# Second attention: key-query scores as two split products with stacked high and low parts

## The chip, the cores and the metric

The kernel runs on one core of a Trainium2 chip. The metric is device time in microseconds (us) of one execution. Five engines share the core: TensorE (PE, its weight loads are listed as PEld), VectorE (DVE), ScalarE (ACT), GpSimd (POOL) and SyncE (SP), which issues most of the DMAs.

## The reference, cut to what matters

The program is two transformer blocks on 512 positions. The second block has two causal attentions of eight heads each, head width 64: one with a forget gate whose cumulated logarithm is added to the scores, and a dilated one with distance penalties. The change touches their scores alone.

```python
def fox_attention(q, k, v, log_f):               # heads 12 to 19 of the kernel
    c = jnp.cumsum(log_f, axis=-1)
    ...
        s = jnp.einsum('bhqd,bhkd->bhqk', qb, k).astype(jnp.float32) * scale   # scale = 64 ** -0.5
        s = s + cq[..., :, None] - c[:, :, None, :]
        s = jnp.where(mask, s, NEG_INF)
        p = jax.nn.softmax(s, axis=-1)
        return jnp.einsum('bhqk,bhkd->bhqd', p.astype(v.dtype), v)

def dilated_window_branch(q, k, v, window, dilation, slopes):   # heads 20 to 27, three patterns in one pass
    s = jnp.einsum('bhrnqd,bhrnkd->bhrnqk', qs, kc).astype(jnp.float32) / math.sqrt(hd)
    ...
    bias = -slopes * (dilation * steps)
    s = jnp.where(valid, s + bias, NEG_INF)
```

A term that depends only on the query drops out of the softmax, so what is left of both biases is one number for each key and head.

## The kernel before

All arrays are fp32. Large projections are not computed as full fp32 products but split: each operand has a high part rounded to the format fp32r and a low part (the value less its high part), and three single-pass products high x high, high x low, low x high are added in one PSUM bank (line 1149). Scores, transposes and value products use full fp32 (lines 1288, 1301, 1317).

The order of all work is a written list, `STEPS`. Every engine walks through this list and does its own share of each step, in this order; semaphores join them. So what stands later in the list can't overtake on the same engine.

The second block's attention numbers its heads a = 12 + j, j = 0 to 15. It works on four query blocks of 128 (qb) and causal keys, so score row qb has (qb + 1) x 128 keys. Iteration j of the loop does, for i = 0 to 3:

- `X(a, i)`: TensorE transposes the probabilities of head a for key block i into a bank; ScalarE copies them to SBUF (line 1630).
- `S(a + 1, i)`: TensorE makes score row i of the next head (line 1288) and adds the mask (line 1290 or 1292); VectorE takes the row maximum (line 1956); ScalarE takes the exponential (line 1428). For heads 12 to 19 ScalarE also sums the row; for later ones VectorE multiplies by a table of counts and sums (line 1965).
- `W(a + 1, i - 1)`: VectorE divides by the row sum (lines 1966, 1967).
- `PV(a, i - 1)`: TensorE's product with the values (line 1317), accumulated over key blocks in one bank, `ob`.

Then follow, for j up to 11, a projection `qk2` (24 split products of 512 columns; the queries or the keys of a pair of heads two pairs ahead), `W(a + 1, 3)`, `PV(a, 3)` and `O(a)`, VectorE's copy of the head's output from `ob` (line 1977). The first value product of the next head waits for this copy:

```python
if kb == 0 and a > 0:
    pe.wait_ge(s_O, O_no[a] - 1)
```

ScalarE empties a `qk2` projection with two instructions, one for each head of the pair, into `Q2` (scaled by 1/8) or `K2`. These hold 65 rows for each of four slots: 64 of the head and one more, 1.0 in `Q2` and the key bias in `K2`, so that one product of 65 rows gives the score with its bias. The bias row comes by one DMA for each head on GpSimd's queue (`key_bias`, line 1010), four at the step `key_biases` ahead of the attention, later ones three to four heads ahead. GpSimd also makes the low parts of the weights for the projections (line 1000), ScalarE their high parts (line 1532, in an iteration behind the copy of transposed block 1).

Score rows and transposes take five PSUM banks in turn. Two banks alternate for projections; a projection waits until the one two before has been emptied.

After the attention come an output projection, a norm, the search for experts and 128 experts' products, which take the rest of the time.

Of the kernel before, what the change touches and what calls it, by code (L numbers as in the profile page):

```python
# [96 lines left out]
def build_schedule():  # L97
# [232 lines left out]
    def qk2(p, s):  # L330
        tile("qk2", 2 * p + s, KD, P)

    qk2(0, 0)
    qk2(0, 1)
    rows(12)
    qk2(1, 0)
    STEPS.append(("W", 12, TB - 1))
    qk2(1, 1)

    def out_part(f, k0, k1):  # L340
# [10 lines left out]
    for j in range(ATT2):  # L351
        a = 12 + j
        for i in range(TB):
            STEPS.append(("X", a, i))
            if j + 1 < ATT2:
                STEPS.append(("S", a + 1, i))
            STEPS.append(("L", a, i))
            if i:
                if j + 1 < ATT2:
                    STEPS.append(("W", a + 1, i - 1))  # L360
                STEPS.append(("PV", a, i - 1))
        if j // 2 + 2 < 8:
            qk2(j // 2 + 2, j % 2)
        if j == 13:
            out_part(0, 0, 3)
        elif j == 14:
            out_part(1, 0, 3)
            out_part(0, 3, 6)
        if j + 1 < ATT2:
            STEPS.append(("W", a + 1, TB - 1))  # L370
        STEPS.append(("PV", a, TB - 1))
        STEPS.append(("O", a))

        if j == ATT2 - 1:
            out_part(1, 3, 6)
        if j in (12, 13, 15):
            STEPS.append(("split", "o", *{12: (0, 3), 13: (3, 6), 15: (6, KD)}[j]))
# [47 lines left out]
def program(nc, t_in, out):  # L425
    build_schedule()
    ctx = ExitStack()
    with ctx:
# [71 lines left out]
        o += T  # L500
        Q2 = region(o, 4 * T, 4)
        rtmp = region(o, T)
# [17 lines left out]
        mq = region(o, 4 * T, 4)  # L520
        K2 = region(o, 4 * T, 4)
        o += 4 * T
# [46 lines left out]
        mv = region(mv_off, MB * T, MB)  # L569
        PT = region(PT_off, 4 * T, 4)  # L570
        hh = place("h_high", HH, [KD, T], F32R)
        hl = place("h_low", 4096, [KD, T], F32R)
# [77 lines left out]
        s_O = sem("head_outputs_done")  # L650
        s_kb = [sem(f"key_bias_in_buffer{i}") for i in range(4)]
        s_fmag = sem("forget_magnitudes_ready")
        s_fch = sem("forget_logs_done")
# [330 lines left out]
        def _(pool):  # L984
# [18 lines left out]
            def key_bias(j):  # L1003
                if j == 0:
                    pool.wait_ge(s_post, post_no[("forget", 0)])
                    pool.wait_ge(s_init2, 1)
                if j >= 4:
                    pool.wait_ge(s_S, s_no[(12 + j - 4, TB - 1)])
                src = zsm[j:j + 1, 2, :] if j < 8 else t_in["bias"][j - 8:j - 7, :]
                pool.dma_start(K2[NOPE:NOPE + 1, j % 4, :], src).then_inc(s_kb[j % 4], 16)  # L1010

            def second_block_buffers(lows):

                pool.wait_ge(s_wlo, lows)
                buffers_set[0] = 1
                pool.wait_ge(s_O, 12)
                nc.gpsimd.memset(Q2[NOPE:NOPE + 1, :, :], 1.0).then_inc(s_init2, 1)

# [15 lines left out]
            for s in STEPS:  # L1034
# [25 lines left out]
                elif s[0] == "X" and 12 <= s[1] < 24 and s[2] == TB - 1:  # L1060
                    key_bias(s[1] - 12 + 4)
            pool.wait_ge(s_kb[3], 16 * 4)

# [39 lines left out]
        def _(pe):  # L1103
# [8 lines left out]
            def proj(n, part=None):  # L1112
# [6 lines left out]
                if n >= 2 and k_begin == 0:  # L1119
                    pe.wait_ge(s_evac, ev(n - 2))  # L1120
                if k_begin:
                    pass
# [133 lines left out]
            def operands(a):  # L1256
# [3 lines left out]
                if a < 12:  # L1260
                    return mq[:, a - HEADS, :], mkT[:, a - HEADS, :], P
                return Q2[:, (a - 12) % 4, :], K2[:, (a - 12) % 4, :], NOPE + 1

# [9 lines left out]
            def S(a, qb):  # L1273
                q, k, K = operands(a)
                if qb == 0:
# [4 lines left out]
                    else:  # L1280
# [3 lines left out]
                        pe.wait_ge(s_evac, ev(pi[("qk2", 2 * p + 1)]))  # L1284
                        pe.wait_ge(s_kb[(a - 12) % 4], 16 * ((a - 12) // 4 + 1))
                ps = score_bank(("S", a, qb))
                N = (qb + 1) * P if a >= 12 else n_keys(a) * P
                last = mm(ps[:, 0:N], q[0:K, qb * P:(qb + 1) * P], k[0:K, 0:N], start=True, stop=(a < 12))  # L1288
                if 12 <= a < 20:
# [128 lines left out]
        def _(act):  # L1418
# [32 lines left out]
            def evac(n):  # L1451
# [57 lines left out]
                elif kind == "qk2":  # L1509
                    p, s = i // 2, i % 2  # L1510
                    if i == 0:
                        act.wait_ge(s_init2, 1)
                    dst = (Q2, K2)[s]
                    scale = (DH ** -0.5, 1.0)[s]
                    for u in range(2):
                        ins = A(dst[0:DH, (2 * p + u) % 4, :], ps[u * DH:(u + 1) * DH, :], ACT.Copy, scale=scale)
                    ins.then_inc(s_evac, 1)
# [125 lines left out]
            for s in STEPS:  # L1643
# [29 lines left out]
                elif s[0] == "post" and s[1] == "forget":  # L1673
                    forget(s[3][0])
                elif s[0] == "split":
                    for k in range(s[2], s[3]):
# [122 lines left out]
        def _(dve):  # L1799
# [143 lines left out]
            def turn(h):  # L1943
# [6 lines left out]
                V.tensor_tensor(x, x, rtmp[R, :], ALU.add).then_inc(s_turn, 1)  # L1950

            def S(a, qb):
                dve.wait_ge(s_S, s_no[(a, qb)])
# [74 lines left out]
            for s in STEPS:  # L2028
# [19 lines left out]
                elif s[0] == "post":  # L2048
                    post(s[1], s[2], s[3])
                elif s[0] == "sum":  # L2050
                    add_squares(s[1], s[2])


# [105 lines left out]

            dve.wait_ge(s_kb[3], 16 * 4)  # L2160
            link(V.tensor_tensor(eq[:, 0:P], ident, iota, ALU.mult))
# [208 lines left out]
```

## Time and profile before

| | |
|---|---|
| median of 3 runs | 2333.74 us (2330.88 to 2334.06) |
| the profiled execution: its own time, its span | 2330.88 us, 2330.9 us |
| TensorE busy | 2250.9 us, 97% of the span |
| VectorE, ScalarE, GpSimd busy | 1289.9, 903.1, 1252.0 us |
| mean granted TensorE clock | 0.991 of full speed |
| second attention, from its first score row to its last value product | 744.58 to about 937.7 us |

A row of a timeline gives the start, the duration and the instruction; a count above one means that neighbouring like instructions are merged. Durations of TensorE's instructions overlap, because they are pipelined: the time that one costs is the distance from its start to the start of the next. A full fp32 product appears as two records. PEclk is the granted TensorE clock, 1.00 for 2.4 GHz and 0.50 for 1.2 GHz.

### The profile page before, as it was taken

Reading aid. Unit: us, or ns where it says so; the run is one execution under the profiler, and the core shown is the slowest. Engines: PE = TensorE matmul, PEld = TensorE weight load, DVE = VectorE, ACT = ScalarE, POOL = GpSimd, SP = SyncE. Lnnn points to the kernel's source line nnn. Section 1 sums busy time; section 2 is a strip of 40 time slices with the busy share of each in tenths; the row PEclk is TensorE's granted clock in tenths of the full one; section 3 lists DMA queues with packets and bytes.
Section 4 is the critical chain, followed back from the end, with each engine's and each line's share of the span. In section 5 each row is a group of like instructions: output and inputs, shape, how many; then the busy total and the mean of one; then the engine's idle time right before and its main releaser. Section 6 shows DMA issues by size and latency. Waiting matters only on the chain.

```text
span 2330.9 us, 29683 instructions
## 1 busy us (share of the span) xinstructions
PE 2250.9 (97%) x9663; PEld 1762.8 (76%) x9670; DVE 1289.9 (55%) x2379; ACT 903.1 (39%) x1427; POOL 1252.0 (54%) x807
## 2 busy tenths in 40 slices
PE   7999899999999999899999999999999999999998
PEld 5666566677767676688888888888887888888887
DVE  5454323214751457588667666322222888888887
ACT  4554444335543444433333333322222333333333
POOL 3432022234534221328888888888887656556553
PEclk9999999999999999999999999999999999999999
DMA  6664123333522110223666666666556899999996
GB/s 234 200 203 148 51 85 104 100 100 132 176 73 83 54 46 28 91 78 64 144 149 142 146 146 148 141 144 145 108 106 161 319 326 349 360 349 354 351 358 243
DMA packets 238226, 392.71 MB, mean 168 GB/s; under 512 B 87201, under 2 KB 161953, under 8 KB 237889
## 3 DMA queue, kind: packets, MB, share of 16 engines
q1 hardware_dynamic: 159808, 324.29, 42.8%
q0 software_dynamic: 78336, 67.45, 14.4%
q8 instruction: 38, 0.62, 0.1%
q14 instruction: 44, 0.35, 0.1%
HBM read 330.60 MB, written 61.01 MB: 168 GB/s over the span
## 4 chain that ended last, share of the span: by engine, by line
PE 56%; DVE 2%; DMA 1%; ACT 0%; issue 0%; POOL 0%; SPq 0%; DVEq 0%; POOLq 0%; ACTq 0%
PE bank L1377 30%; PE bank L1388 22%; PE bank L1149 4%; PE bank L1360 0%; DMA tail<-hidden_of_last_block,low 0%; ACT staged L1428 0%; DMA tail<-gates 0%; DMA hidden_of_last_block<-staged 0%; DVE u_split L2157 0%; DVE low L1863 0%; POOL tail L1076 0%; DVE tail L2089 0%; DVE tail L2124 0%; DVE tail L2122 0%; DVE tail L2125 0%
## 5 line engine op out<-in xcount | busy, mean ns | idle before, releaser
L1028 POOL DMA_INDIRECT gates<-low x384 | 631.9, 1646 | 140.2 <-issue 116.7
L1377 PE MATMUL bank<-h_high,u_tiles_split 128*128 128x512 f32 x2048 | 631.9, 390 | 2.2 <-DVE u_tiles_split L2056 2.2
L1000 POOL TENSOR_TENSOR u_split<-blocks,u_split 128x1024 fp32r<-128x1024 f32 (+1 forms) x102 | 245.0, 2402 | 658.2 <-ACT u_split L1532 625.4
L1149 PE MATMUL bank<-h_high,u_split 128*128 128x512 f32 x1664 | 547.2, 404 | 11.8 <-DVE h_low L1885 7.7
L1388 PE MATMUL bank<-v_split,a_split 128*128 128x512 f32 x2286 | 520.1, 390 | 3.3 <-DVE a_split L2196 3.3
L1388 PEld LDWEIGHTS bank<-v_split,a_split 128*128 128x128 f32 x2286 | 430.0, 188 | 93.4 <-DVE v_split L2193 4.1
L1377 PEld LDWEIGHTS bank<-h_high,u_tiles_split 128*128 128x128 f32 x2048 | 385.3, 188 | 82.4 <-issue 2.4
L1377 PE MATMUL bank<-h_low,u_tiles_split 128*128 128x512 f32 x1024 | 399.1, 390 | 0.0
L1149 PEld LDWEIGHTS bank<-h_high,u_split 128*128 128x128 f32 x1664 | 316.0, 190 | 89.3 <-issue 22.7
L2056 DVE TENSOR_TENSOR u_tiles_split<-tail,u_tiles_split 128x1024 fp32r<-128x1024 f32 x128 | 157.3, 1230 | 362.9 <-ACT u_tiles_split L1713 362.0
L1149 PE MATMUL bank<-h_low,u_split 128*128 128x512 f32 (+1 forms) x704 | 277.2, 394 | 0.0
L1747 ACT CAST v_split<-tail 128x1024 fp32r<-128x1024 f32 x128 | 134.9, 1054 | 294.9 <-PE bank L1388 291.7
L1068 POOL DMA_INDIRECT low<-in_v,low x128 | 142.5, 1113 | 167.0 <-DVE low L2212 136.2
L1377 PEld LDWEIGHTS bank<-h_low,u_tiles_split 128*128 128x128 f32 x1024 | 192.6, 188 | 40.0
L1428 ACT ACTIVATE tail<-bank 128x512 f32<-128x512 f32 x96 | 57.4, 598 | 355.8 <-PE bank L1377 355.8
L2193 DVE TENSOR_TENSOR v_split<-tail,v_split 128x1024 fp32r<-128x1024 f32 x128 | 157.0, 1227 | 67.9 <-ACT v_split L1747 67.9
L1076 POOL DMA_INDIRECT tail<-hidden_of_last_block,low x128 | 168.2, 1314 | 45.5 <-issue 38.4
L2212 DVE SCALAR_TENSOR_TENSOR low<-low,tail 128x1024 f32<-128x1024 f32 x128 | 163.7, 1279 | 1.5 <-DMA low<-in_v,low 1.2
L1149 PEld LDWEIGHTS bank<-h_low,u_split 128*128 128x128 f32 (+1 forms) x704 | 134.2, 191 | 34.2 <-issue 7.5
L1956 DVE TENSOR_REDUCE low<-bank 128x1 f32<-128x512 f32 (+3 forms) x112 | 59.8, 535 | 174.7 <-PE bank L1288 94.5
L1713 ACT CAST u_tiles_split<-tail 128x1024 fp32r<-128x1024 f32 x128 | 133.0, 1040 | 0.8 <-DMA tail<-in_uT 0.5
L1532 ACT CAST u_split<-blocks 128x1024 fp32r<-128x1024 f32 (+1 forms) x112 | 117.4, 1048 | 20.8 <-PE bank L1171 20.4
(219 smaller groups left out, 2366.6 us busy)
## 6 DMA issues: line engine op xcount, KB each, us to landing
tail<-in_uT SPq DMA_DIRECT2D x128, 512.0 KB, 3.8
tail<-in_v SPq DMA_DIRECT2D x128, 512.0 KB, 5.7
gates<-blocks SPq DMA_DIRECT2D x32, 768.0 KB, 5.8
tail<-gates SPq DMA_DIRECT2D x128, 192.0 KB, 5.7
kept_hidden<-tail SPq DMA_DIRECT2D x96, 192.0 KB, 1.9
tail<-kept_hidden SPq DMA_DIRECT2D x96, 192.0 KB, 6.4
blocks<-in_r SPq DMA_DIRECT2D x24, 512.0 KB, 4.1
blocks<-in_conv SPq DMA_DIRECT2D x16, 512.0 KB, 4.4
```

The source lines that it names most:

```text
L1000: nc.gpsimd.tensor_tensor(flat(u, 1)[:, 0:n], ring[:, loads[0] % NW, 0:n], flat(u, 0)[:, 0:n].bitcast(F32), ALU.subtract).then_inc(s_wlo, 1)
L1028: nc.gpsimd.indirect_dma_start(gate_elements, bass.IndirectOffsetOnAxis(ap=expert_no[tb][:, k:k + 1], axis=0), expert_gate[tb][:, k:k + 1] ...
L1068: nc.gpsimd.indirect_dma_start(rows_in[:, k % 4, :], None, v_rows, bass.IndirectOffsetOnAxis(ap=row_no[:, k:k + 1], axis=0))\
L1076: nc.gpsimd.indirect_dma_start(picked[:, k:k + 1], None, hidden_elements, bass.IndirectOffsetOnAxis(ap=hidden_no[:, k:k + 1], axis=0))\
L1149: last = mm(ps[0:m, :], flat(u, part)[:, k * m:(k + 1) * m], x, start=(k == 0 and j == 0), stop=(k == nk - 1 and j == 2))
L1377: last = mm(bank[slot % 2][:, :], U4[:, slot, w, k, :], x[:, k, :], start=(k == 0 and x is hh and w == 0), stop=(k == KD - 1 and w == 1))
L1388: done = mm(bank[2 + 2 * tb + dh][:, :], A2[:, slot, wa, tb * P:(tb + 1) * P], V2[slot // 2][:, slot % 2, wv, dh * T:(dh + 1) * T], start= ...
L1713: nc.scalar.copy(U4[:, slot, 0].rearrange("p k e -> p (k e)"), UR[:, slot, :]).then_inc(s_uhi, 1)
L1747: nc.scalar.copy(V2[slot // 2][:, slot % 2, 0], VR[:, slot, :]).then_inc(s_vhi, 1)
L2056: V.tensor_tensor(U4[:, slot, 1].rearrange("p k e -> p (k e)"), UR[:, slot, :], U4[:, slot, 0].rearrange("p k e -> p (k e)").bitcast(F32), ...
L2193: V.tensor_tensor(V2[slot // 2][:, slot % 2, 1], VR[:, slot, :], V2[slot // 2][:, slot % 2, 0].bitcast(F32), ALU.subtract).then_inc(s_vlo, 1)
L2212: V.scalar_tensor_tensor(sparse, rows_in[:, slot, :], rated[:, bass.ds(k, 1)], sparse, ALU.mult, ALU.add).then_inc(s_axpy, 1)
```

## The change

Queries and keys are now kept as high and low parts, stacked along the contraction. `QA` holds the high part of the query in rows 0 to 63 and its low part in rows 64 to 127; `KA` holds the high part of the key twice. Their product of 128 rows gives high x high and low x high. `QB` (query high part, and two rows of ones) times `KB` (key low part, and two rows with the high and the low part of the key bias) gives high x low and the bias, in 66 rows. Both are single-pass fp32r products, added in the same bank.

ScalarE now empties a projection with four instructions. VectorE makes the low parts in a new step, `qk_low`, of two instructions that read the projection's bank and the high parts. The step stands behind `W(a + 1, 3)` and ahead of `PV(a, 3)` and `O(a)` in the list. The key biases are split by ScalarE and VectorE at the step `key_biases`, for which the distance penalties are first loaded to SBUF, and each head's bias takes two DMAs instead of one.

```diff
+    def qk_low(p, s):
+        STEPS.append(("qk_low", 2 * p + s))
+
     qk2(0, 0)
     qk2(0, 1)
+    qk_low(0, 0)
+    qk_low(0, 1)
     rows(12)
     qk2(1, 0)
     STEPS.append(("W", 12, TB - 1))
+    qk_low(1, 0)
     qk2(1, 1)
+    qk_low(1, 1)
...
         if j + 1 < ATT2:
             STEPS.append(("W", a + 1, TB - 1))
+        if j // 2 + 2 < 8:
+            qk_low(j // 2 + 2, j % 2)
         STEPS.append(("PV", a, TB - 1))
         STEPS.append(("O", a))
...
+        QB = place("queries_high", q2_off, [4, T], F32R)
+        QA = place("queries_stacked", oT_off + 8 * T, [4, T], F32R)
+        KA = place("keys_stacked", k2_off, [4, T], F32R)
+        KB = place("keys_low", R1 + 4 * T, [4, T], F32R)
+        key_bias_parts = place("key_bias_parts", mkT_off, [2, T], F32R)
...
             def key_bias(j):
                 if j == 0:
                     pool.wait_ge(s_post, post_no[("forget", 0)])
+                    pool.dma_start(zsm[32:40, 2, :], t_in["bias"]).then_inc(s_slopes, 16)
+                    pool.wait_ge(s_bias_low, 2)
                     pool.wait_ge(s_init2, 1)
                 if j >= 4:
                     pool.wait_ge(s_S, s_no[(12 + j - 4, TB - 1)])
-                src = zsm[j:j + 1, 2, :] if j < 8 else t_in["bias"][j - 8:j - 7, :]
-                pool.dma_start(K2[NOPE:NOPE + 1, j % 4, :], src).then_inc(s_kb[j % 4], 16)
+                row = j if j < 8 else 32 + j - 8
+                for w in range(2):
+                    pool.dma_start(KB[NOPE + w:NOPE + w + 1, j % 4, :], key_bias_parts[row:row + 1, w, :])\
+                        .then_inc(s_kb[j % 4], 16)
...
                 if n >= 2 and k_begin == 0:
                     pe.wait_ge(s_evac, ev(n - 2))
+                    if PROJ[n - 2][0] == "qk2":
+                        pe.wait_ge(s_qk, PROJ[n - 2][1] + 1)
...
-                last = mm(ps[:, 0:N], q[0:K, qb * P:(qb + 1) * P], k[0:K, 0:N], start=True, stop=(a < 12))
+                if a >= 12:
+                    slot = (a - 12) % 4
+                    mm(ps[:, 0:N], QA[:, slot, qb * P:(qb + 1) * P], KA[:, slot, 0:N], start=True, stop=False)
+                last = mm(ps[:, 0:N], q[0:K, qb * P:(qb + 1) * P], k[0:K, 0:N], start=(a < 12), stop=(a < 12))
...
-                    dst = (Q2, K2)[s]
-                    scale = (DH ** -0.5, 1.0)[s]
                     for u in range(2):
-                        ins = A(dst[0:DH, (2 * p + u) % 4, :], ps[u * DH:(u + 1) * DH, :], ACT.Copy, scale=scale)
+                        slot, src = (2 * p + u) % 4, ps[u * DH:(u + 1) * DH, :]
+                        if s == 0:
+                            A(QA[0:DH, slot, :], src, ACT.Copy, scale=DH ** -0.5)
+                            ins = A(QB[0:DH, slot, :], src, ACT.Copy, scale=DH ** -0.5)
+                        else:
+                            nc.scalar.copy(KA[0:DH, slot, :], src)
+                            ins = nc.scalar.copy(KA[DH:P, slot, :], src)
                     ins.then_inc(s_evac, 1)
...
+                elif s[0] == "key_biases":
+                    act.wait_ge(s_post, post_no[("forget", 0)])
+                    nc.scalar.copy(key_bias_parts[0:8, 0, :], zsm[0:8, 2, :]).then_inc(s_bias_high, 1)
+                    act.wait_ge(s_slopes, 16)
+                    nc.scalar.copy(key_bias_parts[32:40, 0, :], zsm[32:40, 2, :]).then_inc(s_bias_high, 1)
...
+            def qk_low(i):
+
+                n = pi[("qk2", i)]
+                p, of_key = i // 2, i % 2
+                dve.wait_ge(s_evac, ev(n))
+                for u in range(2):
+                    slot, src = (2 * p + u) % 4, pj[n % 2][u * DH:(u + 1) * DH, :]
+                    if of_key:
+                        ins = V.tensor_tensor(KB[0:DH, slot, :], src, KA[0:DH, slot, :].bitcast(F32), ALU.subtract)
+                    else:
+                        ins = V.scalar_tensor_tensor(QA[DH:P, slot, :], src, DH ** -0.5,
+                                                     QA[0:DH, slot, :].bitcast(F32), ALU.mult, ALU.subtract)
+                ins.then_inc(s_qk, 1)
...
+                elif s[0] == "key_biases":
+                    for i, r in enumerate((slice(0, 8), slice(32, 40))):
+                        dve.wait_ge(s_bias_high, i + 1)
+                        V.tensor_tensor(key_bias_parts[r, 1, :], zsm[r, 2, :], key_bias_parts[r, 0, :].bitcast(F32),
+                                        ALU.subtract).then_inc(s_bias_low, 1)
+                elif s[0] == "qk_low":
+                    qk_low(s[1])
```

## Rows read from the trace of the kernel before

**Rows 1.** The page, first part: busy time, share of the span, instructions.
```profile
PE 2250.9 (97%) x9663; PEld 1762.8 (76%) x9670; DVE 1289.9 (55%) x2379; ACT 903.1 (39%) x1427; POOL 1252.0 (54%) x807
```

**Rows 2.** Windows: us, busy time by engine, PEclk, DMA share, GB/s.
```profile
785.63:797.26 11.63, 11.50 (x55) 8.33 (x54) 5.69 (x13) 5.78 (x15) 2.81 (x2) 1.00 0.17 47
...
844.00:855.80 11.80, 11.66 (x56) 8.45 (x56) 7.51 (x21) 5.42 (x12) 2.81 (x2) 1.00 0.13 45
...
912.80:923.25 10.45, 9.95 (x39) 6.69 (x40) 8.07 (x25) 5.14 (x11) 0.00 (x0) 0.84 0.00 0
```

**Rows 3.** TensorE's timeline, one head: start us, us, instruction.
```profile
785.63 0.38 PE L1317 MATMUL bank<-blocks 128*128 128x128 f32 x2
...
786.90 0.60 PE L1288 MATMUL bank<-blocks 65*128 65x256 f32 x2
787.34 0.22 PE L1290 MATMUL bank<-low 128*128 128x128 bf16 x1
787.69 1.13 PE L1317 MATMUL bank<-blocks 128*128 128x512 f32 x2
...
788.87 0.81 PE L1288 MATMUL bank<-blocks 65*128 65x384 f32 x2
789.52 0.22 PE L1290 MATMUL bank<-low 128*128 128x128 bf16 x1
...
790.39 1.02 PE L1288 MATMUL bank<-blocks 65*128 65x512 f32 x2
791.25 0.22 PE L1290 MATMUL bank<-low 128*128 128x128 bf16 x1
...
791.61 0.58 PE L1149 MATMUL bank<-h_high,u_split 128*128 128x512 f32 x1
792.02 0.39 PE L1149 MATMUL bank<-h_low,u_split 128*128 128x512 f32 x1
792.25 0.63 PE L1149 MATMUL bank<-h_high,u_split 128*128 128x512 f32 x2
```

**Rows 4.** ScalarE's timeline, the same head.
```profile
785.83 1.20 ACT L1428 ACTIVATE blocks<-bank 64x512 f32<-64x512 f32 x2 [4.15 <-PE bank L1149]
787.05 0.59 ACT L1630 COPY blocks<-bank 128x512 f32<-128x512 f32 x1
...
788.25 1.07 ACT L1532 CAST u_split<-blocks 128x1024 fp32r<-128x1024 f32 x1
789.20 0.50 ACT L1428 ACTIVATE low<-bank,low 128x256 f32<-128x256 f32 x1
```

**Rows 5.** VectorE's timeline, the same head.
```profile
786.12 0.69 DVE L1977 COPY blocks<-bank 64x512 f32<-64x512 f32 x1 [3.72 <-PE bank L1317]
786.85 0.29 DVE L1956 TENSOR_REDUCE low<-bank 128x1 f32<-128x128 f32 x1
```

**Rows 6.** Groups by form, ScalarE and VectorE, before the second attention.
```profile
L1696 ACT CAST h_high<-low 128x512 fp32r<-128x512 f32 x4 | 2.5, 622 | 2.6 <-DVE low L1863 2.6
...
L1885 DVE TENSOR_TENSOR h_low<-low,h_high 128x512 fp32r<-128x512 f32 x5 | 3.4, 687 | 0.1
```

**Rows 7.** Timelines of TensorE and GpSimd where the second attention begins.
```profile
744.58 0.46 PE L1288 MATMUL bank<-blocks 65*128 65x128 f32 x2 [1.44 <-issue]
...
736.24 2.20 POOL L1010 DMA_DIRECT2D blocks<-low  x4
```

**Rows 8.** Windows of 7 us from the start of a TensorE gap.
```profile
909.49:916.49 7.00, 3.69 (x16) 2.74 (x16) 6.43 (x19) 3.84 (x8) 0.00 (x0) 0.78 0.00 1
942.73:949.73 7.00, 4.22 (x19) 3.54 (x20) 4.04 (x3) 2.79 (x5) 5.03 (x2) 1.00 0.43 138
...
1094.65:1101.65 7.00, 4.84 (x14) 3.90 (x15) 6.04 (x12) 5.81 (x8) 6.08 (x4) 0.76 0.18 3
742.97:749.97 7.00, 5.56 (x17) 3.32 (x17) 4.37 (x10) 4.42 (x11) 2.34 (x1) 0.72 0.23 75
763.13:770.13 7.00, 5.71 (x23) 3.60 (x23) 4.39 (x11) 4.39 (x13) 2.81 (x2) 1.00 0.17 65
```

More of the change, by code:

```diff
@@ L500, in program @@
         o += T
-        Q2 = region(o, 4 * T, 4)
+        q2_off = o
         rtmp = region(o, T)
@@ L520, in program @@
         mq = region(o, 4 * T, 4)
-        K2 = region(o, 4 * T, 4)
+        k2_off = o
         o += 4 * T
@@ L651, in program @@
         s_kb = [sem(f"key_bias_in_buffer{i}") for i in range(4)]
+        s_slopes = sem("distance_penalties_loaded")
+        s_bias_high = sem("key_bias_high_parts")
+        s_bias_low = sem("key_bias_low_parts")
+        s_qk = sem("query_and_key_low_parts")
         s_fmag = sem("forget_magnitudes_ready")
@@ L1016, in second_block_buffers @@
                 pool.wait_ge(s_O, 12)
-                nc.gpsimd.memset(Q2[NOPE:NOPE + 1, :, :], 1.0).then_inc(s_init2, 1)
+                nc.gpsimd.memset(QB[NOPE:NOPE + 2, :, :].bitcast(F32), 1.0).then_inc(s_init2, 1)
             gate_elements = gates.rearrange("e p (t o) -> (e p t) o", o=1)
@@ L1061, in _ @@
                     key_bias(s[1] - 12 + 4)
-            pool.wait_ge(s_kb[3], 16 * 4)
+            pool.wait_ge(s_kb[3], 32 * 4)
             def row_gather(k):
@@ L1261, in operands @@
                     return mq[:, a - HEADS, :], mkT[:, a - HEADS, :], P
-                return Q2[:, (a - 12) % 4, :], K2[:, (a - 12) % 4, :], NOPE + 1
+                return QB[:, (a - 12) % 4, :], KB[:, (a - 12) % 4, :], NOPE + 2
             def score_bank(step):
@@ L1284, in S @@
                         pe.wait_ge(s_evac, ev(pi[("qk2", 2 * p + 1)]))
-                        pe.wait_ge(s_kb[(a - 12) % 4], 16 * ((a - 12) // 4 + 1))
+                        pe.wait_ge(s_qk, 2 * p + 2)
+                        pe.wait_ge(s_kb[(a - 12) % 4], 32 * ((a - 12) // 4 + 1))
                 ps = score_bank(("S", a, qb))
                 N = (qb + 1) * P if a >= 12 else n_keys(a) * P
-                last = mm(ps[:, 0:N], q[0:K, qb * P:(qb + 1) * P], k[0:K, 0:N], start=True, stop=(a < 12))
+                if a >= 12:
+                    slot = (a - 12) % 4
+                    mm(ps[:, 0:N], QA[:, slot, qb * P:(qb + 1) * P], KA[:, slot, 0:N], start=True, stop=False)
+                last = mm(ps[:, 0:N], q[0:K, qb * P:(qb + 1) * P], k[0:K, 0:N], start=(a < 12), stop=(a < 12))
                 if 12 <= a < 20:
@@ L2158, in query_lows @@
                         .then_inc(s_wlo, 1)
-            dve.wait_ge(s_kb[3], 16 * 4)
+            dve.wait_ge(s_kb[3], 32 * 4)
             link(V.tensor_tensor(eq[:, 0:P], ident, iota, ALU.mult))
```

## The prediction, made before the changed kernel was run

> **What bounds the kernel now.** I read the page first: TensorE is busy for 97% of the span, VectorE 55%, ScalarE 39%, GpSimd 54% [rows 1]. A shorter product can therefore pay directly, but an average says nothing of the stage that is edited, so I cut out the second attention with the view of windows. It runs from about 743 to 937 us. One head takes 11.63 us in the first eight and 11.80 us in the second eight, and TensorE is idle for only 0.13 us of either; VectorE works 5.69 and 7.51 us of it, ScalarE 5.78 and 5.42 us [rows 2]. The last heads, which have no query-key projection to fill TensorE, take 10.45 us, of which VectorE works 8.07 us [rows 2]. Then I read one head on each engine's timeline. Counted from the end of the projection (785.63 us, call it 0), TensorE does PV3, the transposes and score rows 0 and 1 of the next head, and has issued them by 1.7 us; its next product, PV0, starts at 2.06 us [rows 3]. That small gap ends when ScalarE, which first empties the projection (0.20 to 1.42 us), has copied the transposed probabilities (1.42 to 2.01 us) [rows 4]. VectorE copies the head's output out at 0.49 to 1.18 us [rows 5], and PV0 may not start before that copy, since both use the same bank; now it is early by 0.9 us. The reader should see how little stands between the end of the projection and PV0: two steps of ScalarE, one of VectorE, all just in time.
>
> **The products.** The full fp32 product leaves two records per score row, one pair replaced by two single-pass products. The old pair takes 0.44 us at 256 keys, 0.65 at 384, 0.86 at 512, by the distance from its start to that of the mask product behind it [rows 3]. A split product of 512 columns starts 0.23 us after the one before (792.02 to 792.25) [rows 3], so two take 0.46 us: 0.40 less. For fewer columns no split product is in the trace. The lower bound is in proportion to the columns, 0.34 and 0.23 us for two (gains of 0.31 and 0.21); the upper bound is that narrow ones get the rate of the old product, so that two cost double, 1.30 and 0.88 us (losses of 0.65 and 0.44). I take proportion, because the wide one is exactly such a ratio. Rows 0 and 1 lie ahead of PV0, where TensorE waits anyway, so only rows 2 and 3 can give anything: 0.31 + 0.40 = 0.71 us per head. The Trainium skill (TensorE: Matmul & The Clock Gate, Back-to-back issue gap) gives N/2.4 + 2.5 ns, thus 0.43 and 0.33 us for two of 512 and 384. By it a head gains 0.03 + 0.01 us more, some 0.6 us over all heads; where they differ, the 0.23 us of this trace decides.
>
> **Emptying the projection.** ScalarE writes each half twice: four instructions for two. The present two take 1.22 us to the next instruction [rows 4]; a 128x512 cast to fp32r takes 0.62 us [rows 6], so the two more cost 1.2 us, and the last ends at 2.6 us instead of 1.4.
>
> **The low parts.** `qk_low` is two VectorE instructions that wait for the last of these four. The nearest row is a subtraction into fp32r of the same width, 0.69 us [rows 6]; two end 1.35 us later, at about 4.0 us. Below that bound I see nothing, as a 64-partition copy costs the same 0.69 us as one of 128 [rows 5, 6]; the other form, with a multiplication, may cost 0.1 us more. The important thing is its place: it stands behind W3 and ahead of the output copy O in VectorE's order. O takes 0.69 us [rows 5] and so ends at 4.6 us, not 1.18. PV0 of the next head waits for it and starts at about 4.65 us: 2.6 us later than now. Behind O are the row maxima of the next head, which began at 1.22 us [rows 5] and now begin at about 4.6; ScalarE's exponential 0 waits for the first of them, and ScalarE's copy of transposed block 1 is queued behind that. The same ordering holds on ScalarE today: its exponential at 789.20 us starts only as the 1.07 us cast ends [rows 4].
>
> **One head, summed.** From PV0 to the projection takes 3.92 us now (787.69 to 791.61) [rows 3]. Less 0.71 it is 3.2. But PV2 needs block 2, and ScalarE has to do exponential 0, copy 1, the cast of weights (1.07), exponential 1 and copy 2 after the first maximum at 4.9 us; this ends near 7.75, while TensorE would be there at 7.6. I take 0.2 us as lost, 0.1 where the row sum is no longer read by ScalarE. So a head costs +2.6 - 0.71 + 0.2 = +2.1 us, about +2.0 in the second eight. W3, which gates the next head's transposes, ends near 13.3 us by the same addition in the second eight, against a projection that now ends at 13.7: close, but hidden. `qk_low` stands in iterations 0 to 11, and each delays the iteration after it: 6 x 2.17 + 6 x 2.0 = 25 us. In iteration 12 there is no projection to hide W3, but its maxima are late by as much, so the 2.0 stays.
>
> **The two ends.** At the start, S(12,0) begins at 744.58 us, behind two evacuations of 1.2 us [rows 7, 4]. Now it waits for four of them (2.4 us) and `qk_low`: it starts 2.5 us later, and its four score rows win back about 1.1 us, +1.4. In iteration 0 the longer evacuation delays PV0 by 1.2 us and rows 2 and 3 give 0.7 back: +0.5. The last three heads have a chain through VectorE (8.07 of 10.45 us) [rows 2], shortened only where it waits for a score row: -1. Key biases: GpSimd's four DMA issues take 2.20 us at 736.24 us [rows 7]. Eight take 4.4, and they now wait for a load, ScalarE and VectorE; I put their end at about 745 us. The weight split behind them ends near 747.5, just ahead of its projection, so I cost this at nothing; uncovered it would be at most 2 to 3 us, once. Later ones are issued three heads ahead. The extra row of the second product (66 partitions for 65) costs nothing, since time goes by columns. Sum: 25 + 1.4 + 0.5 - 1 = +26 us.
>
> **TensorE's clock.** Each of 12 heads gets a gap of about 3 us (1.6 to 4.65). Seven microseconds from the start of a gap show what happens [rows 8]: 7.00 less the busy time is the gap, and PEclk the mean clock. After 3.31 us of gap the mean is 0.78, after 2.16 us 0.76, after 1.44 us of gap among narrow work 0.72; after 2.78 and 1.29 us it is 1.00. 0.76 to 0.78 over 7 us means 3.3 us at the lower level, 1.2 GHz, which loses at most 1.6 us of work, less what falls in a wait. I take three heads in four, 1.3 us each: 12 x 0.75 x 1.3 = 12 us. The bounds are 0 and 12 x 1.7 = 20, some 25 if a fall lasts longer now and then.
>
> The profiled execution has a span of 2330.9 us and is the lowest of the three runs; their median is 2333.7. All later stages hang on TensorE, so they shift whole. 2333.7 + 26 + 12 = **2371.5 us**. A difference under 0.2% (4.7 us) can't be told from no change.
>
> **Rivals.**
> *(A) As summed*, with the clock falling in most heads: 2371.5, own range 2360 to 2382. Chance 0.6.
> *(B) The clock holds* in nearly all heads, since the gap is shorter than 3.31 us and 2.78 us did not disturb it [rows 8]: 2360, range 2352 to 2364. Chance 0.2. Against it: 2.16 us did.
> *(C) Narrow split products run at the old product's rate.* Rows 2 of the score then lose 0.65 instead of winning 0.31, thus 1.0 us for each of 16 heads, and row 1 stays in the gap: +15, 2386. Chance 0.1; the only split width seen is 512.
> *(D) Faster.* If the output copy's delay were hidden, 16 x 0.71 = 11 us would be won: 2323. It needs PV0 to be late by less than 0.7 us instead of 2.6, thus four evacuations, two low parts and the copy within 2.7 us after the projection. The rows give 2.4 us for the evacuations alone. Chance 0.03.
> *(E) A smaller loss*, 2336 to 2352: the evacuations or low parts overlap more than their rows show, each head losing some 1 us. Chance 0.07.
>
> **How the numbers follow.** The range from 2352 to 2388 holds A, B and C, near 0.85 to 0.9. Faster by over 0.2% is D, 0.03; within 0.2% a part of E, 0.02; slower the rest, 0.95.
>
> **What would show it.** In the changed profile: (1) cycles of about 13.7 us (clock held) to 15 us from the second head, and about 10 us in the last heads; (2) TensorE idle ahead of PV0 for about 3 us, ended by VectorE's output copy, not by ScalarE; (3) four evacuations in 2.4 us, two low parts in 1.35 us, then the copy; (4) two records of 0.23 us spacing per 512-key row; (5) PEclk below 1.00 in windows of several heads. The prediction is wrong if PV0 starts under 3.5 us after the projection, if W3 arrives after it, or if the projection waits for the weight split.

## The result, and the profile after

The changed kernel takes 2364.7 us (median of 4 runs, 2363.3 to 2365.5) against 2333.0 us of the kernel before: ratio 1.0138, 95% interval 1.0126 to 1.0151. It is slower by 31.7 us; 2371.5 had been forecast, between 2352 and 2388.

The page of the changed kernel, its span and the busy times that answer to [rows 1]:

```profile
span 2363.7 us, 29785 instructions
...
PE 2244.1 (95%) x9663; PEld 1764.4 (75%) x9670; DVE 1318.1 (56%) x2413; ACT 922.3 (39%) x1461; POOL 1243.7 (53%) x824
```

TensorE works 6.8 us less, over a span that is 32.8 us longer. VectorE has 28 us more and ScalarE 19 us more, and neither is near its limit. So the time went into TensorE's waits and, as shown below, into stretches at its lower clock. To find them, both traces are cut by windows at the same events: the end of the projection ahead of the attention, PV0 of the first head, of the 13th and of the last head. First the kernel before, then the changed one (columns as in [rows 2]):

```profile
0.00:743.14 743.14, 694.53 (x2738) 494.91 (x2738) 297.54 (x410) 339.89 (x567) 239.71 (x128) 0.99 0.42 131
743.14:764.42 21.28, 18.56 (x73) 13.88 (x74) 5.73 (x14) 9.48 (x19) 5.31 (x3) 0.84 0.23 74
764.42:904.86 140.44, 138.90 (x644) 100.65 (x649) 76.84 (x196) 66.78 (x160) 33.15 (x24) 1.00 0.15 43
904.86:934.99 30.13, 25.83 (x110) 17.31 (x112) 23.60 (x68) 14.31 (x32) 2.34 (x1) 0.94 0.03 13
934.99:2330.88 1395.89, 1373.13 (x6100) 1136.07 (x6100) 886.18 (x1692) 472.65 (x652) 971.53 (x652) 0.99 0.72 206
```

```profile
0.00:741.99 741.99, 694.67 (x2738) 494.97 (x2738) 302.10 (x414) 342.12 (x571) 238.52 (x131) 0.99 0.42 132
741.99:765.90 23.91, 16.94 (x73) 13.57 (x73) 8.29 (x20) 12.89 (x24) 8.49 (x6) 0.85 0.22 67
765.90:935.03 169.13, 132.63 (x643) 100.83 (x649) 97.05 (x221) 80.12 (x183) 39.38 (x36) 0.97 0.12 38
935.03:964.14 29.11, 24.67 (x109) 17.81 (x112) 24.08 (x69) 14.57 (x32) 2.35 (x1) 0.88 0.00 1
964.14:2363.70 1399.56, 1375.14 (x6100) 1137.21 (x6100) 886.56 (x1692) 472.60 (x652) 954.95 (x652) 0.99 0.72 205
```

Below, the time from one PV0 to the next is called a cycle. Stage by stage the difference is -1.15, +2.63, +28.69, -1.02 and +3.67 us. Nearly all of it lies in the twelve cycles from the first to the 13th head, 169.13 us instead of 140.44, of which TensorE now idles 36.5 us instead of 1.5.

One of these cycles on TensorE's timeline, answering to [rows 3]. The projection ends at 789.93 us:

```profile
789.93 0.38 PE L1345 MATMUL bank<-blocks 128*128 128x128 f32 x2
...
794.78 1.10 PE L1345 MATMUL bank<-blocks 128*128 128x512 f32 x2 [3.13 <-DVE blocks L2028]
795.72 0.38 PE L1329 MATMUL bank<-low 128*128 128x128 f32 x2
...
796.36 0.86 PE L1345 MATMUL bank<-blocks 128*128 128x384 f32 x2
797.06 0.27 PE L1329 MATMUL bank<-low 128*128 128x128 f32 x1
797.09 0.48 PE L1315 MATMUL bank<-keys_stacked,queries_stacked 128*128 128x512 f32 x1
...
797.72 0.65 PE L1345 MATMUL bank<-blocks 128*128 128x256 f32 x2
```

PV0 starts 4.85 us after the projection, not 2.06, behind 3.13 us of idleness, and what ends this is VectorE's copy of the head's output. ScalarE's and VectorE's timelines for the same head, answering to [rows 4, 5]:

```profile
790.13 0.58 ACT L1547 CAST keys_stacked<-bank 64x512 fp32r<-64x512 f32 x1 [3.20 <-PE bank L1173]
790.73 0.58 ACT L1548 CAST keys_stacked<-bank 64x512 fp32r<-64x512 f32 x1
791.32 0.58 ACT L1547 CAST keys_stacked<-bank 64x512 fp32r<-64x512 f32 x1
791.91 0.58 ACT L1548 CAST keys_stacked<-bank 64x512 fp32r<-64x512 f32 x1
792.51 0.59 ACT L1662 COPY blocks<-bank 128x512 f32<-128x512 f32 x1
795.00 0.37 ACT L1456 ACTIVATE blocks<-bank,low 128x128 f32<-128x128 f32 x1 [1.89 <-DVE low L2007]
```

```profile
792.52 1.39 DVE L1997 TENSOR_TENSOR keys_low<-bank,keys_stacked 64x512 fp32r<-64x512 f32 x2 [4.87 <-ACT keys_stacked L1548]
793.94 0.69 DVE L2028 COPY blocks<-bank 64x512 f32<-64x512 f32 x1
794.67 0.62 DVE L2007 TENSOR_REDUCE low<-bank 128x1 f32<-128x128 f32 x2
```

The reader can add it up: four evacuations from 790.13 to 792.49, two low parts from 792.52 to 793.91, the output copy from 793.94 to 794.63, PV0 at 794.78. In the waits summed by pair, TensorE waited 33.0 us in 11 times for this copy, and in the kernel before never.

Three cycles by windows, an ordinary one of the first eight heads, one of the second eight, and one of the long ones:

```profile
781.04:794.78 13.74, 10.61 (x54) 8.15 (x55) 7.40 (x16) 6.92 (x17) 3.32 (x3) 1.00 0.12 38
...
876.76:890.46 13.70, 10.75 (x54) 8.28 (x55) 9.73 (x25) 6.39 (x13) 3.34 (x3) 1.00 0.12 39
904.37:919.69 15.32, 12.24 (x53) 9.08 (x55) 9.26 (x25) 6.60 (x13) 3.32 (x3) 0.88 0.12 35
```

### The profile page after: what moved, and what is told of

It reads as the page before. It is cut to its first block, busy times and chain, and to the rows that moved or that the text cites. A ratio compares the mean times of both kernels' runs of the same rounds, so it can differ in the third digit from the quotient of the medians.

```text
span 2363.7 us, 29785 instructions
## 1 busy us (share of the span) xinstructions
PE 2244.1 (95%) x9663; PEld 1764.4 (75%) x9670; DVE 1318.1 (56%) x2413; ACT 922.3 (39%) x1461; POOL 1243.7 (53%) x824
## 4 chain that ended last, share of the span: by engine, by line
PE 55%; DVE 2%; DMA 1%; ACT 0%; issue 0%; POOL 0%; SPq 0%; DVEq 0%; POOLq 0%; ACTq 0%
PE bank L1405 29%; PE bank L1416 21%; PE bank L1173 4%; PE bank L1388 0%; ACT staged L1456 0%; DMA tail<-hidden_of_last_block,low 0%; DMA hidden_of_last_block<-staged 0%; DMA tail<-gates 0%; DVE u_split L2215 0%; DVE low L1900 0%; POOL tail L1098 0%; DVE tail L2147 0%; DVE tail L2180 0%; DVE tail L2182 0%; DVE tail L2183 0%
## 5 line engine op out<-in xcount | busy, mean ns | idle before, releaser
L1090 POOL DMA_INDIRECT low<-in_v,low x128 | 132.2, 1033 | 185.2 <-DVE low L2270 150.2
L1345 PE MATMUL bank<-blocks 128*128 128x512 f32 (+1 forms) x208 | 92.2, 531 | 50.1 <-DVE blocks L2028 33.0
```

What stands on the lines that cost most here:

```text
L1090: nc.gpsimd.indirect_dma_start(rows_in[:, k % 4, :], None, v_rows, bass.IndirectOffsetOnAxis(ap=row_no[:, k:k + 1], axis=0))\
```

## The experiments

### The low parts behind the output copy

```diff
         if j + 1 < ATT2:
             STEPS.append(("W", a + 1, TB - 1))
-        if j // 2 + 2 < 8:
-            qk_low(j // 2 + 2, j % 2)
         STEPS.append(("PV", a, TB - 1))
         STEPS.append(("O", a))
+        if j // 2 + 2 < 8:
+            qk_low(j // 2 + 2, j % 2)
```

> The changed kernel with one edit: the step of the low parts stands behind the output copy O instead of ahead of it. Theory (order in the queue): O no longer waits for them, so the first value product PV0 of a head starts when ScalarE has emptied the projection (2.4 us) and copied block 0 (0.6 us), about 3.2 us after the projection instead of 4.6. The row maxima are still behind the low parts, so exponential 0 and the copy of block 1 stay late and take some 0.3 us back: 12 x 1.1 = 13 us less than the changed kernel's 2364.7, near 2352. Rival (the amount of added work on VectorE is what costs, wherever it stands): no change, 2364.7. Rival (the wait is ScalarE's four evacuations, and the low parts are hidden behind them): no change either, and PV0 stays at 4.6 us.

Measured: 2347.5 us, ratio to the kernel before 1.0063 (1.0048 to 1.0079), 17 us less than the changed kernel. The same instructions at another place in the list give back half of the loss, so the amount of VectorE's work is not what costs. The timelines of TensorE, ScalarE and VectorE for one head, where the projection ends at about 788.1 us:

```profile
791.30 1.12 PE L1345 MATMUL bank<-blocks 128*128 128x512 f32 x2 [1.50 <-ACT blocks L1662]
...
790.66 0.58 ACT L1662 COPY blocks<-bank 128x512 f32<-128x512 f32 x1
792.41 0.37 ACT L1456 ACTIVATE blocks<-bank,low 128x128 f32<-128x128 f32 x1 [1.17 <-DVE low L2007]
...
790.67 1.39 DVE L1997 TENSOR_TENSOR keys_low<-bank,keys_stacked 64x512 fp32r<-64x512 f32 x2 [1.40 <-ACT keys_stacked L1548]
792.09 0.62 DVE L2007 TENSOR_REDUCE low<-bank 128x1 f32<-128x128 f32 x2
```

PV0 (791.30) is now 3.2 us behind the projection and follows ScalarE's copy of block 0 (790.66); the wait of 1.50 us is named to ScalarE. The row maxima (792.09) still stand behind the low parts and exponential 0 (792.41) behind them, which is the part that was expected to remain. Cycles are 12.7 to 12.9 us instead of 13.5 to 13.8, in the second eight heads 12.5 and 12.7 instead of 13.7 and 13.9; only the first is longer (13.50 us, PEclk 0.88). The expectation had 1.1 us for each head, the cycles show 0.8 to 1.2; the two late cycles of 15.3 us in the changed kernel are 12.5 and 12.7 us here, which is more than the move explains and comes up again under the filled gap.

### The low parts one head later

```diff
-        if j // 2 + 2 < 8:
-            qk_low(j // 2 + 2, j % 2)
+        if 0 <= j - 1 and (j - 1) // 2 + 2 < 8:
+            qk_low((j - 1) // 2 + 2, (j - 1) % 2)
         STEPS.append(("PV", a, TB - 1))
```

> The changed kernel with the low parts of a projection made one head later, behind W3, while TensorE works on the next projection. The last use allows it: the pair is needed two heads later. Theory (order): neither O nor the maxima wait for them; only ScalarE's two more evacuations stay, so PV0 starts 3.2 us after the projection and nothing is given back: 12 x 1.4 for PV0 and 12 x 0.3 for what ScalarE no longer delays, 20 us less than 2364.7, near 2345. Rival (amount of work): 2364.7. Rival (ScalarE): 2364.7.

Measured: 2339.6 us, ratio 1.0033 (1.0020 to 1.0046). Behind the first (13.51 us, PEclk 0.88) the cycles are 12.0 to 12.3 us. The run is 5 us faster than expected: the late maxima cost more than the 0.3 us put down for them, and the two long late cycles are gone here too. PV0 is where it was in the last experiment, with a wait of 1.51 us for ScalarE's copy, so the 0.4 to 0.7 us by which the cycles are shorter is what the late maxima had cost. The rest of the loss, 0.3 to 0.5 us for each head against the kernel before, is ScalarE's two additional evacuations less what the products give.

### Both one head later

ScalarE empties the projection in a step of its own, one iteration later and behind exponential 3, and the low parts stand as in the last experiment.

```diff
+        if 0 <= j - 1 and (j - 1) // 2 + 2 < 8:
+            STEPS.append(("qk_evac", j - 1 + 4))
         if j + 1 < ATT2:
             STEPS.append(("W", a + 1, TB - 1))
...
-                if s[0] == "proj":
-                    evac(s[1])
+                if s[0] == "qk_evac":
+                    evac(pi[("qk2", s[1])])
+                elif s[0] == "proj":
+                    if PROJ[s[1]][0] != "qk2" or PROJ[s[1]][1] < 4:
+                        evac(s[1])
```

> As the one before, and ScalarE empties the projection one head later too, behind exponential 3. The other bank takes the next projection meanwhile. Theory: nothing of the conversion is left between the projection and PV0, which starts as soon as TensorE has issued score row 1, about 1.6 us after the projection. The products then pay: 12 heads x (0.35 gap + 0.55 for rows 2 and 3 as measured) = 11 us under the kernel before, less 1 in the last heads, plus 2.7 at the start: near 2324, faster than both. Rival (the split products bring nothing, since their measured spacing is wider than forecast): the gap alone is won, 4 us, 2332 with the start. Rival (emptying late makes the score rows of the next pair wait): every second head loses 0.5 us or more, 2330 and over, with a wait ahead of S(a, 0) in the trace.

Measured: 2327.7 us, ratio 0.9976 (0.9967 to 0.9985): faster than both kernels, though not by as much as the 2324 expected. Six of the twelve cycles are 10.41 us (10.59 in the second eight heads), five are 10.8 to 11.4, and the first, 11.94, lies partly at the lower clock (PEclk 0.87). The five are longer because TensorE waits there for the low part of the keys. A row of its timeline, the first score row of a pair:

```profile
863.45 0.30 PE L1317 MATMUL bank<-keys_stacked,queries_stacked 128*128 128x128 f32 x1 [0.58 <-DVE keys_low L2002]
```

In the first eight heads the wait is shorter and the view puts it down to "issue", but there too the score row starts 0.36 us after the end of the low parts (798.99 and 798.63 us), as it does here (863.45 and 863.09). So both the theory and its last rival were right, each for about half of the heads. The last three heads missed as well: 1 us less than before was expected, and they take 31.99 us instead of 30.13. There is no projection left to hide W3, and ahead of the 14th head's first transposes TensorE waits 4.24 us for VectorE's division instead of 3.30.

### The kernel before with the late evacuation

```diff
+        if 0 <= j - 1 and (j - 1) // 2 + 2 < 8:
+            STEPS.append(("qk_evac", j - 1 + 4))
         if j + 1 < ATT2:
             STEPS.append(("W", a + 1, TB - 1))
```

with the same edit on ScalarE as above, and nothing of the split products.

> The kernel before with one edit: its two evacuations of a projection are made one head later, behind exponential 3. No split products. Theory: PV0 starts at 1.7 us instead of 2.06, 12 x 0.35 = 4 us less than 2333.0, near 2329; the difference between this and the kernel with everything moved is then what the products bring, 8 us less 2.7 for the start. Rival (PV0's wait is something else): 2333.

Measured: 2329.95 us, ratio 0.9992 (0.9983 to 1.0002), which doesn't separate it from the kernel before. The cycles do: 11.30 us instead of 11.63, TensorE busy in all of it, and in the second eight heads 11.44 instead of 11.80. Against this kernel the split products can be read by themselves, since TensorE sets both cycles: 11.30 less 10.41 is 0.89 us for each of the first eight heads. In the second eight the split cycles are 10.59 and, in the version with ScalarE's evacuation before exponential 3 below, 10.69, so it is 0.8 us.

### The two products in the other order

```diff
-                if a >= 12:
-                    slot = (a - 12) % 4
-                    mm(ps[:, 0:N], QA[:, slot, ...], KA[:, slot, 0:N], start=True, stop=False)
-                last = mm(ps[:, 0:N], q[...], k[0:K, 0:N], start=(a < 12), stop=(a < 12))
+                last = mm(ps[:, 0:N], q[...], k[0:K, 0:N], start=True, stop=(a < 12))
+                if a >= 12:
+                    slot = (a - 12) % 4
+                    last = mm(ps[:, 0:N], QA[:, slot, ...], KA[:, slot, 0:N], start=False, stop=False)
```

> The kernel with everything moved one head later, with the two products of a score row in the other order: the 66-row product (query high, key low) first, the stacked one of 128 rows second. In the changed kernel the first of a 512-column pair has 0.31 us to the second, which has 0.24 us to the mask; at 384 columns 0.26 and 0.18. Theory (position: the first fp32r product behind a full fp32 product or transpose pays some 0.08 us more): the 66-row product now has the 0.31 and the stacked one 0.24, no change in time, 2327.7. Rival (the stack of 128 rows costs more than 66 rows): the first has 0.24, the second 0.31, again with no change in the sum.

Measured: 2327.1 us, ratio 0.9975 (0.9966 to 0.9985), no change from the kernel that it edits. TensorE's timeline of it, transpose block and score row 3 of a head:

```profile
790.12 0.27 PE L1331 MATMUL bank<-low 128*128 128x128 f32 x1
790.14 0.48 PE L1315 MATMUL bank<-keys_low,queries_high 66*128 66x512 f32 x1
790.46 0.40 PE L1318 MATMUL bank<-keys_stacked,queries_stacked 128*128 128x512 f32 x1
790.70 0.23 PE L1320 MATMUL bank<-low 128*128 128x128 bf16 x1
```

The 66-row product, now first, has 0.32 us to the next, and the stacked one 0.24 us to the mask. It is the position, not the 128 rows. But the row above it shows that the theory's surplus is not paid: the transpose starts at 790.12 and the product behind it at 790.14, while a transpose otherwise takes 0.11 us. The record of the product starts early and holds the transpose's time. The five rows of the previous kernel (both one head later) let one measure from outside, from the transposes to the next value product:

```profile
789.17 1.08 PE L1347 MATMUL bank<-blocks 128*128 128x512 f32 x2
790.09 0.38 PE L1331 MATMUL bank<-low 128*128 128x128 f32 x2
...
790.74 0.86 PE L1347 MATMUL bank<-blocks 128*128 128x384 f32 x2
791.44 0.27 PE L1331 MATMUL bank<-low 128*128 128x128 f32 x1
...
792.09 0.65 PE L1347 MATMUL bank<-blocks 128*128 128x256 f32 x2
```

Row 2 with its transposes takes 0.65 us (790.09 to 790.74), row 3 also 0.65 (791.44 to 792.09).

### Filling the gap

```diff
             def PV(a, kb):
+                if kb == 0 and 13 <= a < 24:
+                    n = pi[("qk2", a - 13 + 4)]
+                    pe.wait_ge(s_evac, ev(n - 1))
+                    pe.wait_ge(s_qk, a - 13 + 4)
+                    for t in range(10):
+                        mm(pj[(n + 1) % 2][:, :], hh[:, 0, 0:P], hh[:, 0, :], start=True, stop=True)
                 pe.wait_ge(s_Ph, x_no[(a, kb)])
```

> The changed kernel, with ten 512-column fp32r products of no use (into the idle projection bank, read by nothing) issued ahead of PV0 in iterations 1 to 11, where TensorE waits 2.9 to 3.1 us for the output copy. Ten take 2.3 us, so they end inside the gap. Theory (the clock falls are a cost of their own, on top of the wait): heads of 15.1 to 15.3 us disappear, all heads are at 13.5 to 13.9, and about 3 to 5 us less than 2364.7 is taken, near 2361. Rival (the long heads come from elsewhere, a late weight split or a late W3): they stay, 2364.7. Rival (the products delay PV0): more than 2364.7, with PV0 later than 4.7 us after the projection.

Measured: 2362.3 us, ratio 1.0127 (1.0112 to 1.0143). Its interval overlaps that of the changed kernel, so the time by itself settles nothing. The profile does for the heads. The ten products end before PV0:

```profile
790.00 2.56 PE L1338 MATMUL bank<-h_high 128*128 128x512 f32 x10
793.33 1.10 PE L1351 MATMUL bank<-blocks 128*128 128x512 f32 x2 [0.77 <-DVE blocks L2034]
```

The gap at 793.33 is down to 0.77 us and the cycles are unchanged (13.55 and 13.75 in turn). The two long late cycles, 15.32 and 15.34 us, are 13.70 and 13.90, with PEclk 1.00 in both; the first one, whose gap ahead of it was not filled, is still 15.05. So the long cycles are the clock's, and the rival (late work) is out. These two cycles are 3.1 us shorter; the median is 2.4 us lower, which the intervals don't separate from nothing.

### ScalarE's evacuation before exponential 3

```diff
             STEPS.append(("X", a, i))
+            if i == TB - 1 and 0 <= j - 1 and (j - 1) // 2 + 2 < 8:
+                STEPS.append(("qk_evac", j - 1 + 4))
             if j + 1 < ATT2:
                 STEPS.append(("S", a + 1, i))
```

instead of behind the loop over i.

> The kernel with everything moved one head later, but ScalarE empties the projection ahead of exponential 3 instead of behind it, where it sat idle for 1.8 us. In that kernel every second head waited 0.4 to 0.6 us ahead of its first score row for the low part of the keys, and its cycle was 10.8 to 11.4 us against 10.4 to 10.6. Theory: exponential 3 and W3 come 0.6 us later, hidden behind the projection, and the keys are ready: all heads at 10.4 to 10.6 us, 6 x 0.6 = 3 to 4 us less than 2327.7, near 2324. Rival (W3 becomes late instead, in the second eight heads above all): the wait moves to the transposes, no gain.

Measured: 2324.6 us, ratio 0.9967 (0.9955 to 0.9979). Behind the first (11.95 us, PEclk 0.87) the cycles of the first eight heads are 10.41 to 10.46 us, those of the second eight 10.59 and 10.69, and TensorE is busy for the whole of them. The waits ahead of the score rows are gone.

### The first pair under a projection

```diff
     for i in range(1, 8):
         tile("v2", i, 2, T)
-    STEPS.append(("key_biases",))
+        if i == 4:
+            STEPS.append(("key_biases",))
...
     qk_low(0, 0)
+    qk2(1, 0)
     qk_low(0, 1)
     rows(12)
-    qk2(1, 0)
-    STEPS.append(("W", 12, TB - 1))
-    qk_low(1, 0)
+    STEPS.append(("qk_evac", 2))
     qk2(1, 1)
-    qk_low(1, 1)
+    STEPS.append(("W", 12, TB - 1))
+    qk_low(1, 0)
```

The late evacuation and late low parts of the loop now begin with the last projection ahead of it.

> The last kernel with the start of the attention reordered: the key biases are made three value projections earlier, and the projection of the second pair's queries runs ahead of the first head's score rows, so that it covers the emptying and the low parts of the first pair (a gap of 4.2 us, followed by 6.8 us at the lower clock). Theory: the gap of 4.2 us and up to 3.4 us of the clock are won, 5 to 7 us less than the last kernel, near 2318. Rival (GpSimd's weight split for that projection is not ready earlier): a wait takes the place of the gap, less than 2 us won.

Measured: 2316.6 us, ratio 0.9933 (0.9919 to 0.9946), 8 us less than the last. The gap of 4.2 us and the low clock after it are gone, and so is the gap of 2.80 us ahead of the first PV0 (now 0.19). A new wait came, followed by a shorter stretch at the lower clock (mean 0.76 over 7 us), and GpSimd's and TensorE's timelines show where from:

```profile
716.36 0.73 POOL L1027 DMA_DIRECT2D low<-in_bias  x1
720.09 3.95 POOL L1034 DMA_DIRECT2D keys_low<-key_bias_parts  x8 [3.00 <-DVE key_bias_parts L2112]
724.00 4.91 POOL L1021 TENSOR_TENSOR u_split<-blocks,u_split 128x1024 fp32r<-128x1024 f32 x2
...
726.55 0.47 PE L1198 MATMUL bank<-u_split,h_high 128*128 128x512 f32 x1 [2.86 <-POOL u_split L1021]
```

GpSimd issues the load of the penalties (716.36), waits 3.0 us for it and for the two engines that split it, issues eight DMAs (3.95 us), and only then makes the weight low part for which TensorE waits 2.86 us.

### The key biases spread out

```diff
-        if i == 4:
+        if i == 3:
             STEPS.append(("key_biases",))
+        if i in (4, 5, 6, 7):
+            STEPS.append(("key_bias", i - 4))
...
-                    for j in range(4):
-                        key_bias(j)
+                    pool.wait_ge(s_post, post_no[("forget", 0)])
+                    pool.dma_start(zsm[32:40, 2, :], t_in["bias"]).then_inc(s_slopes, 16)
+                elif s[0] == "key_bias":
+                    key_bias(s[1])
```

> The last kernel, where GpSimd's key-bias block (a load, 3.0 us of waiting for it and for the split, then eight DMA issues of 3.95 us) sat ahead of a weight split and left TensorE waiting for 2.86 us. Now the load is issued one value projection earlier and each head's two DMAs stand behind a value projection of their own. Theory: the 2.86 us wait goes and nothing replaces it, 2 to 3 us less than 2316.6, near 2314. Rival (the weight split is late for another reason, ScalarE's cast): the wait stays, 2316.6.

Measured: 2313.1 us, ratio 0.9915 (0.9901 to 0.9928). The wait of 2.86 us is gone. This version is 0.85% faster than the kernel before and 2.2% faster than the changed one, with the same two products for each score row. Between the profiled executions of this version and of the kernel before lie 20.4 us: 9.1 ahead of the first PV0, 13.6 in the twelve cycles (126.86 us instead of 140.44), and the last three heads and the rest give 2.3 back.

Not all of that belongs to the split products. The kernel before with the late evacuation takes 136.45 us for the twelve cycles, so 4.0 of the 13.6 us are the late evacuation's and 9.6 the products'. For the 9.1 us ahead of the first PV0 there is no such control: no run gives the kernel before this start, so how much of it that kernel could have had too isn't shown.

## Why the prediction was right, point by point

**What bounds the kernel** held: TensorE in the heads, and the short stretch from the end of the projection to PV0 as the place where it breaks.

**The products.** Forecast 0.71 us for rows 2 and 3. Measured from outside, from the transposes to the next value product, with these rows of the kernel before:

```profile
788.65 0.38 PE L1301 MATMUL bank<-low 128*128 128x128 f32 x2
...
789.58 0.86 PE L1317 MATMUL bank<-blocks 128*128 128x384 f32 x2
790.28 0.27 PE L1301 MATMUL bank<-low 128*128 128x128 f32 x1
...
791.31 0.65 PE L1317 MATMUL bank<-blocks 128*128 128x256 f32 x2
```

Row 2 takes 0.93 us before (788.65 to 789.58) and 0.64 after (795.72 to 796.36), row 3 1.03 (790.28 to 791.31) and 0.66 (797.06 to 797.72), together 0.66 won. The proportional price for narrow products was right, and the rival with the old rate was wrong: even a row of 256 keys is won, 0.83 to 0.65 us, though it pays only when the gap behind it is closed. That is how the 0.89 us of the experiments comes about: the kernel before with the late evacuation and the one with both moved differ by 0.04, 0.18, 0.28 and 0.38 us in the four rows.

**Evacuation, low parts, copy.** Forecast for their ends 2.6, 4.0 and 4.6 us after the projection, and PV0 at 4.65; measured 2.56, 3.98, 4.70 and 4.85. With the queries it is 4.65, because two of the four copies then follow each other after 0.50 instead of 0.60 us. The price of a low part on 64 partitions was right (1.39 us for two, forecast 1.35), although the row of 128 partitions with which the prediction compares its copy of 64 is a subtraction and not a copy. That order in a queue did it, and not the amount of work, is shown by the two experiments that move the same instructions and give 17 and 25 us back. The Trainium skill (TensorE: Matmul & The Clock Gate, the table at its head) calls the queues of ScalarE and VectorE strictly first in, first out; the trace agrees, the copy's input having been ready since 790.3 us while it started at 793.94.

**One head.** Forecast +2.17 and +2.0 us. Nine of the twelve cycles are of ordinary length: together 123.33 us after and 105.18 before, 2.02 us each. In two places the sum was less exact than this looks. Its terms, 2.6 - 0.71 + 0.2, give 2.09 and not the 2.17 that was multiplied. And the 0.2 us lost behind PV0, in ScalarE's chain up to block 2, did not come: from PV0 to the projection it is 3.23 us (794.78 to 798.01) with 0.66 won by the rows, out of 3.92 before, so nothing was lost there. PV0 after a projection of keys was later by as much (4.85 instead of 4.65), so the two offset each other. W3 stayed hidden, as worked out.

**The ends.** From the projection to the first PV0 +2.63 us, forecast 1.4 + 1.2 up to this point. The last heads -1.02, forecast -1; this agreement is partly luck, because the changed kernel has more of the lower clock in these heads (mean 0.88 instead of 0.94, by which an estimated 1.7 us of TensorE's time at most were lost besides). The key biases cost nothing at their place in the changed kernel; they did as soon as the start was tightened.

**The clock** is the term that was mis-sized. Forecast: three gaps in four followed by the lower level, 9 falls, 12 us. Seven microseconds from the start of a gap, by windows of the changed kernel (as in [rows 8]):

```profile
763.10:770.10 7.00, 4.20 (x12) 2.40 (x12) 4.12 (x9) 4.65 (x11) 3.30 (x3) 0.76 0.17 65
791.65:798.65 7.00, 3.87 (x17) 2.50 (x18) 5.05 (x10) 4.65 (x13) 1.80 (x1) 1.00 0.14 56
...
916.81:923.81 7.00, 4.12 (x12) 2.37 (x12) 4.11 (x11) 3.79 (x9) 2.27 (x1) 0.76 0.16 61
...
971.88:978.88 7.00, 4.22 (x11) 3.38 (x11) 4.01 (x3) 2.79 (x5) 4.99 (x2) 0.65 0.40 143
```

Gaps of 2.80 and 2.88 us were followed by the lower clock (mean 0.76), one of 3.13 us was not (1.00). In the heads it fell behind 4 gaps of 13, and three cycles of 15.1 to 15.3 us instead of 13.6 to 13.9 are the cost: 45.80 us less 35.26 before is 10.54, less 3 x 2.02 leaves 4.5. A gap of 2.78 us that both kernels have ahead of the output projection gave 1.00 before [rows 8] and 0.65 here; the work behind it, up to the product behind TensorE's next gap (0.86 us in both), takes 37.93 us (974.66 to 1012.59) instead of 35.04 (945.51 to 980.55), which is 2.9 of the 3.67 us after the attention. The same gap in the kernel before with the late evacuation is followed by 0.65 as well, so a fall there needs no split products. So some 7 us are the clock, four tenths of it outside the stage that was edited, and the mechanism is 12 x 2.02 + 2.63 - 1.02 = 25.8 us, where 26 had been summed. The 1.15 us ahead of the attention and the last 0.8 us behind it are left without a cause. Which gap is followed by a fall can't be said from these traces. Behind its first 25 us the trace of the kernel before has eight gaps of 2.1 to 4.0 us, of which seven were followed by a fall, more than the three in four that was taken; in the heads it was 4 in 13. With the clock holding in most heads it went by rival B's mechanism there, and the total came out between its forecast and that of A.

## What to carry to other kernels

When an edit adds work to engines with half of their time free, what counts is what stands behind it in each queue: here 2.5 us of conversions more ahead of a 0.7 us copy held the next value product back by 2.6 to 2.8 us and cost 2.0 us net for each head, and moved one head later they left TensorE no wait in the cycles that have a projection. Look how many iterations lie between a result and its first reader before placing the work that makes it. And put the gain (0.8 to 0.9 us a head) where TensorE really sets the cycle, by closing the small waits around it first.

## What had not been expected of the hardware

Behind a full fp32 transpose, the record of an fp32r product starts 0.02 us after the transpose's, which otherwise takes 0.11 us, and the product then seems to take 0.31 us where 0.23 is its rate. The order of the two products makes no difference to it. Distances between neighbouring records of different kinds should be checked against a distance from outside.

VectorE's scaling of 128x256 values took 1.45 us in the kernel before and 1.92 us in the changed one, where it starts earlier within GpSimd's 2.38 us subtraction, against 0.35 us when GpSimd is idle. In both it ended 0.15 us after GpSimd's instruction (785.52 against 785.36 us in the changed kernel, 791.89 against 791.74 before). No run moved one of the two alone, so the cause isn't shown. It cost nothing here, since W3 has slack.
